# Two transformer blocks on one core: a reordered hybrid mixer, key attention in steps inside the delta rule, scaled rows in place of diagonals

## The reference, cut to what matters

```
y = f(x * (1 + scale) + shift);  x = layer_norm(ALPHA * x + (1 + gate) * y, ln_g, ln_b)
layer 0: ffn, hybrid mixer, ffn        layer 1: ffn, MLA, ffn
hybrid: a_q,a_k,a_v,i_q,i_k,i_w,b_qkv,b_a,b_b,b_z = split(u @ w_in)
  out_a = attention of 8 heads over the 64 keys per query with the largest
          I[t,s] = sum_h w[t,h] relu(i_q[t,h] . i_k[s]),   ALiBi penalty, softmax
  out_b = gated delta rule: conv of 4 taps, silu, unit q and k, chunks of 64 tokens:
          T = (I + strict_lower(beta k k^T decay))^-1;  u = T (beta v);  w = T (beta k e^g)
          v_new = u - w S;  o = (q e^g) S + A v_new;  S = e^g_last S + k_dec^T v_new
  out   = concat(out_a, rms_norm(out_b) * silu(b_z)) @ w_out
```

## Time and profile before

| | us |
|---|---|
| median of 3 runs | 1720.02 (1712.66 to 1722.41) |
| the profiled execution: its time | 1713.82 |
| its span | 1711.9 |
| PE busy | 1499.6 (88%) |
| DVE busy | 1165.2 (68%) |
| ACT busy | 868.9 (51%) |
| mean granted clock of PE | 0.935 |

### The profile page before, as it was taken

The page is one execution under the profiler, slowest core; times in us unless marked ns, Lnnn a source line. Parts: engine busy times, 40 slices in busy tenths (PEclk is TensorE's granted clock), DMA queues, the critical chain, the costliest instruction groups (busy, mean ns, idle before and its releaser), DMA issues.

```text
span 1711.9 us, 23732 instructions
## 1 busy us (share of the span) xinstructions
PE 1499.6 (88%) x8963; PEld 1292.6 (76%) x8963; DVE 1165.2 (68%) x2082; ACT 868.9 (51%) x1601; POOL 0.2 (0%) x4
## 2 busy tenths in 40 slices
PE   2999989967788999989998569799996998699987
PEld 1788879957666888768887567578885996599856
DVE  5888879738648887788888554586668444464364
ACT  0555454641355554455554447555555964485463
POOL 0000000000000000000000000000000000000000
PEclk8999989987888999989999689899998999999999
DMA  9898858520023888458875070276654550436000
GB/s 365 286 326 320 292 189 277 184 69 1 1 99 121 319 317 296 162 208 318 319 276 176 28 249 1 98 245 220 200 172 148 173 185 1 148 106 202 40 1 25
DMA packets 198413, 306.50 MB, mean 179 GB/s; under 512 B 11458, under 2 KB 160028, under 8 KB 198300
## 3 DMA queue, kind: packets, MB, share of 16 engines
q1 hardware_dynamic: 195472, 302.51, 51.9%
q10 hardware_dynamic: 2828, 2.48, 0.4%
HBM read 303.91 MB, written 1.05 MB: 178 GB/s over the span
## 4 chain that ended last, share of the span: by engine, by line
PE 77%; DVE 13%; ACT 6%; issue 2%; ACTq 1%; PEld 1%; PEldq 0%; DVEq 0%
PE bank L852 19%; PE bank L779 12%; PE bank L780 12%; PE bank L781 12%; PE bank L851 8%; PE bank L1302 3%; PE bank L1289 2%; PE bank L1319 2%; DVE zT L354 1%; DVE wp_lo L1087 1%; PE bank L372 1%; PE bank L854 1%; ACT arena L1354 1%; DVE w_lo L902 1%; DVE uT L573 1%
## 5 line engine op out<-in xcount | busy, mean ns | idle before, releaser
L852 PE MATMUL bank<-u_hi_lo,w_hi 128*128 128x512 f32 x1408 | 501.3, 400 | 11.9 <-DVE u_hi_lo L448 9.1
L851 PE MATMUL bank<-u_hi_lo,w_lo 128*128 128x256 f32 x1232 | 348.2, 283 | 1.7 <-DVE u_hi_lo L448 1.7
L902 DVE TENSOR_TENSOR w_lo<-weight_ring,w_hi 128x1024 fp32r<-128x1024 f32 x264 | 307.8, 1219 | 12.6 <-ACT w_hi L872 12.1
L852 PEld LDWEIGHTS bank<-u_hi_lo,w_hi 128*128 128x128 f32 x1408 | 261.2, 190 | 65.6 <-issue 10.1
L872 ACT CAST w_hi<-weight_ring 128x1024 fp32r<-128x1024 f32 x264 | 260.4, 1046 | 25.9 <-DMA weight_ring<-in_ffn_w_gate_dram 15.9
L851 PEld LDWEIGHTS bank<-u_hi_lo,w_lo 128*128 128x128 f32 x1232 | 235.0, 191 | 14.8 <-DVE u_hi_lo L448 6.9
L1087 DVE TENSOR_TENSOR wp_lo<-weight_ring,wp_hi 128x1024 fp32r<-128x1024 f32 (+4 forms) x149 | 167.5, 1164 | 46.5 <-ACT wp_hi L1054 46.2
L779 PE MATMUL bank<-src_hi,wp_hi 128*128 128x256 f32 (+1 forms) x632 | 187.9, 297 | 5.0 <-DVE src_lo L448 5.0
L780 PE MATMUL bank<-src_lo,wp_hi 128*128 128x256 f32 (+1 forms) x632 | 181.8, 288 | 0.0
L781 PE MATMUL bank<-src_hi,wp_lo 128*128 128x256 f32 (+1 forms) x632 | 181.5, 287 | 0.0
L1054 ACT CAST wp_hi<-weight_ring 128x1024 fp32r<-128x1024 f32 (+4 forms) x149 | 143.7, 1007 | 57.1 <-PE bank L781 55.1
(11 more groups left out here) (336 smaller groups left out, 2222.6 us busy)
## 6 DMA issues: line engine op xcount, KB each, us to landing
weight_ring<-in_mod_w_dram SPq DMA_DIRECT2D x72, 1024.0 KB, 6.9
weight_ring<-in_ffn_w_gate_dram SPq DMA_DIRECT2D x44, 1024.0 KB, 5.6
weight_ring<-in_ffn_w_up_dram SPq DMA_DIRECT2D x44, 1024.0 KB, 5.4
weight_ring<-in_ffn_w_down_dram SPq DMA_DIRECT2D x44, 1024.0 KB, 8.2
weight_ring<-in_hyb_w_in_dram SPq DMA_DIRECT2D x16, 1024.0 KB, 8.1
weight_ring<-in_w_in_e_dram SPq DMA_DIRECT2D x16, 1024.0 KB, 5.5
weight_ring<-in_w_in_o_dram SPq DMA_DIRECT2D x13, 1024.0 KB, 5.4
weight_ring<-in_hyb_w_out_dram SPq DMA_DIRECT2D x4, 1024.0 KB, 5.0
```

What stands on the lines that cost most here:

```text
L851: nc.tensor.matmul(bank[:, 0:SEQ], w[1], u[:, 0:SEQ], start=False, stop=False, skip_group_check=True)
L852: last = nc.tensor.matmul(bank[:, :], w[0], u, start=kt == 0, stop=kt == KT - 1, skip_group_check=True)
L902: nc.vector.tensor_tensor(part_view(wl, n, part), raw, part_view(wh, n, part).bitcast(F32), ALU.subtract).then_inc(w_lo.sem, w_lo.up())
```

## The change

Five things change.

1. **Opening.** The silu of `c` is issued after three of ACT's loads rather than after all; `c` and the rows of `mod_w` are laid over partitions as 8 neighbouring rows each; x is loaded by SP ahead of the seventh weight tile; unit 0 is reduced before x is turned; the first casts and low halves stand behind the first quarter of the input.
2. **Hybrid projections.** The six jobs of the delta rule alternate with gates, queries and keys. The index products go in four steps of two units ahead of jobs 4 to 7, their relus into `act_mid` 4 to 7, their sums into DVE's iterations 6 to 9. The sums of squares stand ahead of jobs 8, 10, 12 and 14, their squares in `act_mid` 7, 9, 11, 13. The choice of keys, with all eight rounds and `selection`, is in DVE's iterations 10 to 18. The decays of group 1 stand ahead of job 16.
3. **Delta rule.** The key attention runs in 12 steps inside it: one in each of five levels (between `tbt` and `update`), one after `uw`, the others in the chunks. Group 1 goes first up to the levels.
4. **No separate attention** stage in the hybrid mixer.
5. **Rows scaled.** In `attention`, DVE multiplies the probabilities by the row weights in place, over the keys' width, and PE turns them with transposes. A joint pair is added on DVE, and PE turns one matrix.

The diff, cut to its core:

```diff
             def act(self, act, split_hi, hi):
-                split_hi(0)
                 act.wait_ge(mod_taken.sem, 2)
                 for c in range(4):
                     self.high(act, hi, c)
+                    if c == 0:
+                        split_hi(0)
...
                     for st, k in pair.tiles(a):
-                        for hh in range(2):
-                            c = st if pair.joint else 2 * hh + st
-                            last = nc.tensor.matmul(PB[2 + u % 2][0:k, c * P:(c + 1) * P],
-                                                    pr[:, u % 2, hh, st * P:st * P + k], dg[:, u % 2, hh, :],
...
+                        for hh in range(1 if pair.joint else 2):
+                            c = 2 * hh + st
+                            last = nc.tensor.transpose(PB[2 + u % 2][0:k, c * P:(c + 1) * P],
+                                                       pr[:, u % 2, hh, st * P:st * P + k], ident)
...
+            def dots(pe, i):
+                pe.wait_ge(job_taken.sem, job_taken.base + 3)
+                if i == 0:
+                    pe.wait_ge(small_ready.sem, small_ready.base + 2)
+                else:
+                    pe.wait_ge(i_relu.sem, i_relu.base + i)
...
             for t in range(6):
+                jobs += [qkv_job(t), others[t]]
...
-            pe_pre = {3: turn_small, 11: lambda pe: head_sum(pe, 0), 12: lambda pe: [head_sum(pe, t) for t in (1, 2, 3)],
-                      14: dots_of(0, 1), 15: dots_of(2, 3), 16: dots_of(4, 5)}
-            act_mid = {4: take_small, 7: silus(0), 8: silus(1), 9: silus(2), 10: silus(3, 4), 11: silus(5),
-                       12: gate_exps, 13: logs, 14: roots, 15: relus_of(0, 1), 16: relus_of(2, 3)}
+            pe_pre = {2: turn_small, 8: lambda pe: head_sum(pe, 0), 10: lambda pe: head_sum(pe, 1),
+                      12: lambda pe: head_sum(pe, 2), 14: lambda pe: head_sum(pe, 3), 16: decays_ahead}
+            act_mid = {3: take_small, 9: act_steps(silu_of=1, gates=True, root_of=0),
+                       11: act_steps(silu_of=2, root_of=1), 13: act_steps(silu_of=3, root_of=2),
+                       15: act_steps(silu_of=4, root_of=3)}
+            for i in range(4):
+                pe_pre[4 + i] = lambda pe, i=i: dots(pe, i)
+                act_mid[4 + i] = act_steps(relu_of=i, silu_of=0 if i == 3 else None)
+                dve_at[6 + i] = dve_steps(index=i)
+            projections(jobs, uT, post=post, slots=4, n_units=1, head=head, x_rows_of=(0, 1), pe_pre=pe_pre,
+                        act_mid=act_mid, act_post={16: lambda act: silu(act, 5)}, dve_at=dve_at)
...
+            def attend_pe(pe, i):
+                if i < 8:
+                    n, a = keys[i]
+                    if i >= 1:
+                        pe.wait_ge(biased.sem, biased.base + 2 * i)
+                    for hh in range(2):
+                        r = slice(64 * hh, 64 * hh + 64)
+                        last = nc.tensor.matmul(PB[2 + hh][:, 0:SEQ], aqT[r, n, a * P:(a + 1) * P], akT[r, n, :],
+                                                start=True, stop=True)
+                    last.then_inc(logits_ready.sem, logits_ready.up())
+                if 2 <= i < 10:
+                    u = i - 2
+                    pe.wait_ge(rows_ready.sem, rows_ready.base + u + 1)
...
+            def attend_dve(dve, i):
...
+                    dve.wait_ge(logits_ready.sem, logits_ready.base + i + 1)
+                    if i >= 1:
+                        dve.wait_ge(probs_ready.sem, probs_ready.base + i)
+                    for hh in range(2):
+                        nc.vector.tensor_tensor_reduce(
...
-                top_rounds(2 if lv < 3 else 1)
+                attend()
                 for g in range(2):
                     @block.vector
                     def update(dve):
```

More of the change, by code:

```diff
@@ L1767, in hybrid @@
             first = len(jobs)
-            for t in range(6):
-                jobs.append(proj_T(w_in, c_qkv + t * 256, 256, conv_in[:, 2 * t:2 * t + 2, 3:SEQ + 3]))
-            for t in range(2):
-                tile, k, k0, fill, _ = proj_T(w_in, c_z + t * 256, 256, None)
-                jobs.append((tile, k, k0, fill, lambda copy, bank, t=t: nc.scalar.activation(
-                    zgT[:, 2 * t:2 * t + 2, :].rearrange("p k t -> p (k t)"), bank[:, :], ACT.Silu)))
-            for t in range(2):
-                jobs.append(scaled_T(w_in, t * 256, aqT[:, 2 * t:2 * t + 2, :], table("q_scale")[:, 2 * t:2 * t + 2]))
@@ new lines, in gate_job @@
+            def gate_job(t):
+                tile, k, k0, fill, _ = proj_T(w_in, c_z + t * 256, 256, None)
+                return tile, k, k0, fill, lambda copy, bank: nc.scalar.activation(
+                    zgT[:, 2 * t:2 * t + 2, :].rearrange("p k t -> p (k t)"), bank[:, :], ACT.Silu)
+            others = [gate_job(t) for t in range(2)]
+            others += [scaled_T(w_in, t * 256, aqT[:, 2 * t:2 * t + 2, :], table("q_scale")[:, 2 * t:2 * t + 2])
+                       for t in range(2)]
@@ new lines, in dve_steps, with run @@
+            def dve_steps(index=None, gates=False, scale=None, rounds=0, last=False):
+                def run(dve):
+                    if index is not None:
+                        if index == 0:
+                            chunks_seen(dve)
+                        index_sum(dve, index)
+                    if gates:
+                        gate_values(dve)
+                    if scale is not None:
+                        head_scale(dve, scale)
+                    for _ in range(rounds):
+                        top_round(dve)
+                    if last:
+                        selection(dve)
+                return run
@@ L1931, in hybrid @@
-            after_diffs = []
-            for g in range(2):
+            keys = [(n, a) for n in range(4) for a in range(TT)]
+            att_room = qkv.rearrange("p k t -> p (k t)")
+            lg = att_room[:, 0:512].rearrange("p (h s) -> p h s", h=2)
+            pr = att_room[:, 512:1536].rearrange("p (b h s) -> p b h s", b=2, h=2)
+            pT = scratch.rearrange("p (b h q) -> p b h q", b=2, h=4)
+            nmax, rsum, rinv = (arena.take(3 * 2, "p (b h) -> p b h", b=3) for _ in range(3))
@@ L1933, in decay_diffs, with _ @@
+            @block.tensor
+            def _(pe):
+                decays(pe, 0)
+            after_diffs = [0, 0]
+            for g in (1, 0):
                 @block.vector
@@ L1942, in decay_diffs @@
                     ins.then_inc(gstep[g].sem, gstep[g].up())
-                after_diffs.append(gstep[g].count)
-            top_rounds(1)
-            for g in range(2):
+                after_diffs[g] = gstep[g].count
+            for g in (1, 0):
                 @block.scalar
@@ L2001, in turn_kv @@
                     last.then_inc(gstep[g].sem, gstep[g].up())
-                after_turn.append(gstep[g].count)
-            for g in range(2):
+                after_turn[g] = gstep[g].count
+            for g in (1, 0):
                 @block.vector
```

416 lines of the change are left out of this document (229 added, 187 removed).

## The result

The changed kernel takes 1729.51 us (median of 6 runs, 1728.29 to 1730.58), the kernel before 1717.70 (6 runs, 1712.66 to 1722.41) on the same chips. The ratio is 1.0069, interval 1.0042 to 1.0096: slower by 0.7%. The forecast was 1710 and faster; 1729.5 lies within its range, but the sign is wrong. The profiled executions are 1728.4 and 1711.9 in span, 16.5 apart; before ran in some executions near 1713 and in others near 1720, and its profile is of the first kind, so of the 16.5 a part is that.

A forecast was written before the change was run, and what follows sets the result against it. TensorE, busy 88% of the span, was taken as the bound, with transfers limiting the opening. Terms −4.6 + 17.4 − 6.3 + 21 + 8 − 26 − 18 made −8.5 us, forecast 1710, range 1690 to 1732.

The forecast's parts named there:

- Step 7: Rows scaled in the attentions of MLA, even and odd layer: shorter turns save 18 us, from −25 to −8.
- a fall of the clock at 4%: Rival, chance 0.04: transposes don't keep the clock up, attention stages turning with them run at 1.2 GHz; +60, 1770.
- Step 2: Hybrid projections: waits ahead of index products and sums of squares grow, clock falls; +17.4 us, from +10 to +22.
- The term for the clock: Hybrid projections: with the waits the clock falls to 0.50 for a job's part more than before; +4 us.
- Step 4: Levels of the inverse: `update` waits behind the key attention's logits; +21 us, from +15.5 to +36.
- The forecast period of 10.4: Levels: us from one level's first `bt` to the next, 6.13 before plus 4.3 that nothing covers.
- The rival of levels slowed by the clock: Chance 0.24: idle time keeps TensorE at 1.2 GHz through levels (+36) and chunks (+12), 19 us more; 1730.
- Steps 3, 5 and 6: Projections' end to first level, −6.3 us; tail and chunks with seven steps more, +8; separate attention gone, −26.0.
- step 5: Tail and chunks: +1.3 us for the step behind `uw`, 2.3, 2.4 and 1.5 for the chunks; taken as +8.
- Step 1: Opening: earlier silu lets sums follow the tiles, less casts now on the path; −4.6 us, between −7 and 0.

The follow-up runs named there:

- turn_twice: The changed kernel with each transpose of the shared attention issued twice into the same place; 1730.41 us in one run.
- mended: The changed kernel with update_first and jobs_apart together, and transposes issued twice in the even and odd layer's attention only; median 1684.86 us, ratio to before 0.9805.
- mended_single: As mended, but with single transposes everywhere as in the changed kernel; median 1686.62 us, ratio to before 0.9812.
- jobs_apart: The changed kernel with index products ahead of jobs 4, 6, 8, 10 and sums of squares ahead of 9, 11, 13, 15; span 1704.5 us.
- update_first: The changed kernel with VectorE's part of each level's key-attention step behind `update`, ScalarE's behind the next `take_x`; span 1714.5 us, levels 34.2 for 58.8.

## Why the prediction was wrong

**Step 7 failed: -18 forecast, -1.2 measured.** It counted TensorE's time saved in turns, at full clock, and bounded it at -8. That the rest of TensorE's work would run slower once the turns were short stood in the sum at nothing.

In the even and the odd layer this is what happened (+1.5 and +0.8 us for -5 and -9.6). TensorE, busy 71 and 82% before, did less, and its granted clock fell from 0.94 to 0.71 and 0.74, which made its other products longer by more than the turns had saved. turn_twice and the pair mended and mended_single show the clock as the cause: with nothing changed but the repetition of each transpose, it is back, and 2.5 to 3.0, or 2.1 to 2.8, us with it.

MLA kept clock 1.00 and gained 3.5 for 5.6. A pair takes 4.33 for 4.1 forecast. The base of that forecast was too high to begin with: 38.71 / 8 = 4.84 shares the stage's busy time out, while from pair to pair were 4.73 us. And the wait was another: I expected ScalarE's copy and took VectorE's scaled rows to cost "about the same" as the diagonals; it is for these rows that TensorE waits 3.4 us where it waited 1.0. The even and the odd layer have the same longer waits, and I had no term for them.

I had a fall of the clock at 4% under the rule that transposes don't count, priced it at +60, and dismissed it with the earlier trace rows. Those rows do speak against the rule. The Trainium skill's page "TensorE: Matmul & The Clock Gate", section "Part 4: PE-mode transpose", says that a transpose doesn't count as the engine being busy in the same way; this case contradicts it: with each transpose doubled the clock was 0.89 and 0.95, and MLA with single ones ran at 1.00. But the earlier trace rows are 64 transposes in a row, with nothing between them; that they don't say what a stage with pauses does, I missed. The earlier trace rows had the idle time: 9.3 of 65.9 us in the odd stage before anything was taken away.

**Step 2, +17.4 forecast, +22.5 measured.** The waits were right: 23.2 forecast, 23.6 measured, each within 1.0 us (the reduce's 2.5 was 3.5). The term for the clock was too small: 4 forecast, and 8.7 are left of the 22.5 without the 11.3 of longer waits and the 2.5 forecast for moved products. jobs_apart, where 9.4 went beside the waits, agrees.

**Step 4, +21 forecast, +24.9 measured,** for the reason given: update behind logits. The term that was mis-sized is the clock. I had put 2.5 us for it in all; against update_first, which does the same work, it is 10.5 (a mean of 0.78 means 1.2 GHz for 44% of the time). The idle time beside it, 14.1 us, is 10.6 more than before (3.5). The forecast period of 10.4 was built on the shortest one before, levels 4 to 5 (6.1); the same one is now 12.0. The rival of levels slowed by the clock came true in part, 24.9 of its 36; its sign did not, for in levels 2 to 4 the first group's `bt` still takes 1.16 to 1.26 us, and it is the second group's that takes 2.08.

**Steps 3, 5 and 6** came within 1.4 us (step 5's terms add up to 7.5, where the sum took 8). **Step 1** was -3.7 for -4.6: the first product stands at 42.18, 4.9 sooner and near the 42.5 forecast, but the first product with down weights only 3.4 sooner (57.91 for 61.34). The second quarter of the input, for which TensorE now waits 1.12 us, stands between them.

**The sum.** Steps 2 and 4 lack 9 us, step 7 lacks 17, and 26.2 is the distance between -8.5 and +17.7. In three of the terms the same thing was too small or missing: what the granted clock takes from TensorE's other work. That the total still fell within the range is luck: it lies beside the 1730 of the rival "the clock in the levels", but of that rival's 19 us steps 4 and 5 gave only about 5, and the rest came from steps 7 and 2.

## What to carry to other kernels

Where TensorE is not nearly always busy, taking work from it can make the stage slower. It need not: MLA with TensorE busy 81% kept clock 1.00, and the odd layer with 80% fell to 0.74. The busy share alone doesn't tell which it will be. So look at the granted clock along the stage, from its start, and give the sum a term for the stage's other products at 1.2 GHz. Where a step is laid inside a serial chain, it goes behind the chain's own instruction on VectorE and ScalarE; it was the place ahead of `update` and the next `take_x` that cost 25 us, not the step. A product fed by an iteration whose casts wait for the end of a job belongs one job later than the first at which it could stand; look then at what that delays behind it (5.7 of 29.5 us here).

## What the runs showed of the hardware

Repeating each transpose, useless work, made the odd attention 2.5 us and the even 3.0 us shorter. Behind five of the eight waits of 2.3 to 3.8 us in the projections the granted clock was 0.50 for some 3 to 7 us, behind the other three it stayed at 1.00; the seven of them that jobs_apart took away, 20.1 us, cost 29.5. The same instructions in the same order took 3 to 7 us more or less in kernels that differ only further on: the stretch between projections and first `bt` ran at 0.98 in one and 0.75 in the other, 19.8 against 24.0 us. What sets that is open; single totals are uncertain by as much, which is why the stages are compared here.
